# The second mixer's delta rule with its two token halves in one stage each

## What is computed

```
def step(state, inp):
    r_t, w_t, k_t, v_t, a_t, b_t = inp
    sa = jnp.einsum('bhvk,bhk->bhv', state, a_t)
    state = (state * w_t[:, :, None, :] + sa[..., None] * b_t[:, :, None, :]
             + v_t[..., None] * k_t[:, :, None, :])
    return state, jnp.einsum('bhvk,bhk->bhv', state, r_t)

_, y = lax.scan(step, jnp.zeros((B, H, d, d), jnp.float32), xs)
```

## Time and profile before

| what | value |
|---|---|
| median of 3 runs | 2688.8 us |
| the three runs | 2682.73, 2688.80 and 2691.91 us |
| the profiled execution's own time | 2688.18 us |
| its span | 2686.0 us |
| mean granted clock of TensorE in it | 0.96 |
| TensorE busy | 2472.5 us, 92% of the span |
| VectorE busy | 1835.3 us, 68% |
| ScalarE busy | 1307.8 us, 49% |
| GpSimd busy | 517.4 us, 19% |

### The profile page before, as it was taken

One profiled execution on the slowest core, in us unless ns is written; L12 is line 12 of the kernel. 1 busy time (PEld: TensorE's weight loads), 2 busy tenths in 40 slices (PEclk: granted clock), 3 DMA queues, 4 the chain that ended last, 5 costly groups with the idle time before them and its releaser, 6 DMA issues. The chain is left out here.

```text
span 2686.0 us, 47036 instructions
## 1 busy us (share of the span) xinstructions
PE 2472.5 (92%) x17864; PEld 2248.3 (84%) x17864; DVE 1835.3 (68%) x3790; ACT 1307.8 (49%) x1990; POOL 517.4 (19%) x328
## 2 busy tenths in 40 slices
PE   5698999999999999778999999999999987887999
PEld 4588999987878788668999998788887966786998
DVE  6775888768777776763888857666666456554754
ACT  3345664546544445454665456455545543044433
POOL 0001676623000000200576753000000020000000
PEclk8799999999999999789999999999999988899999
DMA  8755777772788776624677773577774531042554
GB/s 353 270 174 153 183 184 181 194 244 43 256 256 261 252 249 200 240 95 145 184 180 181 186 181 75 169 218 215 217 215 137 182 119 56 14 138 71 172 160 154
DMA packets 200517, 480.59 MB, mean 179 GB/s; under 512 B 54448, under 2 KB 87728, under 8 KB 199760
## 3 DMA queue, kind: packets, MB, share of 16 engines
q1 hardware_dynamic: 150960, 431.75, 50.7%
q10 hardware_dynamic: 12576, 47.29, 4.9%
q0 software_dynamic: 36864, 0.15, 3.5%
HBM read 461.15 MB, written 17.96 MB: 178 GB/s over the span
## 5 line engine op out<-in xcount | busy, mean ns | idle before, releaser
L278 DVE TENSOR_TENSOR weight_low<-weight_raw,weight_high 128x1024 fp32r<-128x1024 f32 x732 | 893.1, 1222 | 410.9 <-ACT weight_high L272 405.8
L272 ACT ACTIVATE weight_high<-weight_raw 128x1024 fp32r<-128x1024 f32 x732 | 773.8, 1059 | 690.9 <-DMA weight_raw<-peer_v_dram 344.3
L382 PE MATMUL bank<-h_high,weight_high 128*128 128x256 f32 x3424 | 981.5, 287 | 71.7 <-DVE h_low L537 21.7
L382 PE MATMUL bank<-h_low,weight_high 128*128 128x256 f32 x3424 | 978.3, 286 | 0.0
L382 PE MATMUL bank<-h_high,weight_low 128*128 128x256 f32 x3424 | 977.7, 286 | 0.0
L382 PEld LDWEIGHTS bank<-h_high,weight_high 128*128 128x128 f32 x3424 | 666.9, 195 | 84.1 <-issue 75.5
L382 PEld LDWEIGHTS bank<-h_low,weight_high 128*128 128x128 f32 x3424 | 666.8, 195 | 0.0
L382 PEld LDWEIGHTS bank<-h_high,weight_low 128*128 128x128 f32 x3424 | 666.7, 195 | 0.0
L1171 POOL DMA_INDIRECT gate_table<-pick_expo,pick_spot x256 | 474.3, 1853 | 667.3 <-DVE pick_expo L1273 390.6
L1452 PE MATMUL bank<-weight_high,act_high 128*128 128x512 f32 x1024 | 319.5, 393 | 9.8 <-DVE act_low L1519 6.1
L1452 PE MATMUL bank<-weight_low,act_high 128*128 128x512 f32 x1024 | 317.0, 391 | 0.0
(11 more groups left out here) (348 smaller groups left out, 2610.0 us busy)
## 6 DMA issues: line engine op xcount, KB each, us to landing
weight_raw<-peer_u_dram SPq DMA_DIRECT2D x256, 512.0 KB
weight_raw<-peer_v_dram SPq DMA_DIRECT2D x256, 512.0 KB
kept<-ada_later_dram ACTq DMA_DIRECT2D x54, 512.0 KB, 4.7
gate_table<-kept ACTq DMA_DIRECT2D x8, 2048.0 KB, 18.1
weight_raw<-peer_w_q_dram SPq DMA_DIRECT2D x32, 512.0 KB
kept<-gate_table SPq DMA_DIRECT2D x256, 64.0 KB, 4.3
weight_raw<-w_in_dram SPq DMA_DIRECT2D x32, 512.0 KB
weight_raw<-mlp_w_up_dram SPq DMA_DIRECT2D x32, 512.0 KB
```

What stands on the lines that cost most here:

```text
L272: self.nc.scalar.activation(self.high[:, slot, :], self.raw[:, slot, :], ACT.Identity) \
L278: eng.tensor_tensor(self.low[:, slot, :], self.raw[:, slot, :], self.high[:, slot, :].bitcast(F32), ALU.subtract) \
L382: mm = self.nc.tensor.matmul(out, w, x, start=(start and i == 0), stop=(stop and i == 2), skip_group_check=skip)
```

## The change

The function `tile` and its loop go. Each of the three blocks now exists once and works on both halves, so that six blocks become three. The tensors NT, LT, RB, RK, M1, inv and inv_T hold 16 heads instead of 8 (8t + h), and `both` moves to `spots[5]`, where a_in and b_out lie, which are no longer needed by then.

- Scores: the loop over the eight groups runs for t = 0 and then for t = 1, into the same eight banks. Group for group, TensorE waits before it writes a bank again until VectorE has read it. VectorE's 16 operations keep their size. GpSimd makes 32 copies in this block.
- Levels: the two groups that alternate are now the two halves with 8 heads each, instead of two groups of four heads within a half. A product is 16 matmuls instead of 8, and a VectorE operation 128x512 instead of 128x256. Six levels are gone through once instead of twice.
- Final products: every step is done for half 0 and then for half 1 before the next step begins, in other banks.

The number of matmuls, their size and their operands are the same. The core of the diff:

```diff
-    def tile(t):
...
+    with nc.Block() as block:
+        @block.tensor
+        def _(pe):
+            for t in range(TT):
                 for n, (left, right, _, _) in enumerate(kinds):
                     for g in range(2):
+                        if t:
+                            pe.wait_ge(out_ready.sem, out_ready.at(2 * n + g + 1))
                         for h in range(g, 8, 2):
...
-                        nc.vector.tensor_tensor(dst[:, g:8:2, :], half4(2 * n + g), mask(which), ALU.mult)
...
+                        dve.wait_ge(full.sem, full.at(8 * t + 2 * n + g + 1))
+                        nc.vector.tensor_tensor(product_of[:, 8 * t + g:8 * t + 8:2, :], half4(2 * n + g), mask(which, 4), ALU.mult) \
+                            .then_inc(out_ready.sem, 1)
+
+        @block.gpsimd
+        def _(pool):
+            for g in range(TT * 8):
+                nc.gpsimd.tensor_copy(inv[:, g, :], eye2)
+                nc.gpsimd.tensor_copy(inv_T[:, g, :], eye2)
...
+            def product(bank, left, right, t):
                 for h in range(8):
                     for c in range(2):
...
+                        mm = nc.tensor.matmul(core.bank[bank + 3 * t][rows(c), hc(h)], left[rows(c), 8 * t + h, :],
+                                              right[rows(c), 8 * t + h, :], start=True, stop=True, skip_group_check=True)
+                return mm
+
+            for level in range(6):
+                for t in range(TT):
+
+                    if level:
+                        pe.wait_ge(out_ready.sem, out_ready.at(4 * (level - 1) + 2 + t + 1))
+                    product(0, NT, inv, t).then_inc(full.sem, 1)
+                for t in range(TT):
+
+                    pe.wait_ge(out_ready.sem, out_ready.at(4 * level + t + 1))
+
+                    if 0 < level < 5:
+                        product(1, inv_T, M1, t)
+                    product(2, M1, inv_T, t).then_inc(full.sem, 1)
+
+        @block.vector
+        def _(dve):
+            for level in range(6):
+                for t in range(TT):
+                    dve.wait_ge(full.sem, full.at(4 * level + t + 1))
+                    nc.vector.tensor_tensor(M1[:, heads_of(t), :], eight(3 * t), mask(level, 8), ALU.mult).then_inc(out_ready.sem, 1)
+                for t in range(TT):
+                    dve.wait_ge(full.sem, full.at(4 * level + 2 + t + 1))
+                    own = heads_of(t)
+                    if level < 5:
+                        nc.vector.tensor_tensor(inv[:, own, :], inv[:, own, :], eight(1 + 3 * t) if level else M1[:, own, :], ALU.add)
+                    nc.vector.tensor_tensor(inv_T[:, own, :], inv_T[:, own, :], eight(2 + 3 * t), ALU.add).then_inc(out_ready.sem, 1)
...
+            for t in range(TT):
+                pe.wait_ge(out_ready.sem, out_ready.at(t + 1))
                 for g in range(2):
                     for h in range(4 * g, 4 * g + 4):
...
-                pe.wait_ge(out_ready.sem, out_ready.at(3))
+            for t in range(TT):
+                pe.wait_ge(out_ready.sem, out_ready.at(2 + 2 * t + 2))
                 for c in range(2):
+                    out = core.bank[2 + 2 * t + c]
...
+            for t in range(TT):
                 for c in range(2):
+                    out = core.bank[(6, 7, 0, 1)[2 * t + c]]
                     for h in range(8):
...
+            for chunk in range(CHUNKS):
+                sums = core.bank[2 + chunk]
+                dve.wait_ge(full.sem, full.at(6 + chunk + 1))
...
+            for chunk in range(CHUNKS):
+                dve.wait_ge(full.sem, full.at(10 + chunk + 1))
+                sums = core.bank[(6, 7, 0, 1)[chunk]][:].rearrange("p (o n k) -> p o n k", o=2, n=4)
...
-    for t in range(TT):
-        tile(t)
```

More of the change, by code:

```diff
@@ L2314, in rwkv @@
     full, out_ready = sig("products_ready"), sig("products_kept")
-    def tile(t):
[L2318 to L2329, removed]
+    half = lambda h: slice(64 * (h % 2), 64 * (h % 2) + 64)
@@ new lines, in rwkv @@
+    hc = lambda h: slice(h * 64, (h + 1) * 64)
+    rows = lambda c: slice(CHUNK * c, CHUNK * (c + 1))
+    of_chunk = lambda t, c: slice(t * P + CHUNK * c, t * P + CHUNK * (c + 1))
+    mask = lambda i, heads: masks[:, i, :].unsqueeze(1).to_broadcast([P, heads, CHUNK])
+    kinds = [(b_out, a_in, NT, 6), (k_out, a_in, LT, 6), (b_out, r_in, RB, 7), (k_out, r_in, RK, 7)]
+    bank4 = lambda i: core.bank[i][:].rearrange("p (h k) -> p h k", h=4)
+    eight = lambda i: core.bank[i][:].rearrange("p (h k) -> p h k", h=8)
@@ L2333, in _ @@
                             for c in range(2):
-                                mm = nc.tensor.matmul(core.bank[2 * n + g][rows(c), hc(h // 2)], left[half(h), h // 2, of_chunk(c)],
-                                                      right[half(h), h // 2, of_chunk(c)], start=True, stop=True, skip_group_check=True)
+                                mm = nc.tensor.matmul(core.bank[2 * n + g][rows(c), hc(h // 2)], left[half(h), h // 2, of_chunk(t, c)],
+                                                      right[half(h), h // 2, of_chunk(t, c)], start=True, stop=True, skip_group_check=True)
@@ L2345, in _ @@
[L2345 to L2388, removed]
@@ L2396, in _ @@
+    full.close(16)
+    out_ready.close(16)
+    with nc.Block() as block:
+        @block.tensor
+        def _(pe):
+            def product(bank, left, right, t):
                 for h in range(8):
                     for c in range(2):
[L2398 removed]
+                        mm = nc.tensor.matmul(core.bank[bank + 3 * t][rows(c), hc(h)], left[rows(c), 8 * t + h, :],
[11 more added lines that the diff above has]
+                    product(2, M1, inv_T, t).then_inc(full.sem, 1)
+        @block.vector
+        def _(dve):
+            for level in range(6):
[8 more added lines that the diff above has]
+                    nc.vector.tensor_tensor(inv_T[:, own, :], inv_T[:, own, :], eight(2 + 3 * t), ALU.add).then_inc(out_ready.sem, 1)
@@ L2399, in _ @@
+    full.close(24)
+    out_ready.close(24)
+    with nc.Block() as block:
+        @block.tensor
+        def _(pe):
+            for t in range(TT):
+                for h in range(8):
+                    for c in range(2):
+                        mm = nc.tensor.matmul(core.bank[t][rows(c), hc(h)], LT[rows(c), 8 * t + h, :], v_tok[rows(c), t, hc(h)],
                                               start=True, stop=True, skip_group_check=True)
                 mm.then_inc(full.sem, 1)
+            for t in range(TT):
@@ L2404, in _ @@
                         for c in range(2):
-                            nc.tensor.matmul(core.bank[1 + g][rows(c), at + 64:at + P], inv_T[rows(c), h, :], a_tok[rows(c), t, hc(h)],
-                                             start=True, stop=True, skip_group_check=True)
-                pe.wait_ge(out_ready.sem, out_ready.at(1))
+                            nc.tensor.matmul(core.bank[2 + 2 * t + g][rows(c), at + 64:at + P], inv_T[rows(c), 8 * t + h, :],
+                                             a_tok[rows(c), t, hc(h)], start=True, stop=True, skip_group_check=True)
+            for t in range(TT):
+                pe.wait_ge(out_ready.sem, out_ready.at(t + 1))
                 for g in range(2):
@@ L2423, in _ @@
                         at = slice(T + (h // 2) * 64, T + (h // 2) * 64 + 64)
-                        nc.tensor.matmul(core.bank[3 + c][half(h), at], b_tok[rows(c), t, hc(h)], both[rows(c), h, 0:64],
+                        nc.tensor.matmul(out[half(h), at], b_tok[rows(c), t, hc(h)], both[rows(c), 8 * t + h, 0:64],
                                          start=True, stop=False, skip_group_check=True)
-                        mm = nc.tensor.matmul(core.bank[3 + c][half(h), at], k_tok[rows(c), t, hc(h)], v_tok[rows(c), t, hc(h)],
+                        mm = nc.tensor.matmul(out[half(h), at], k_tok[rows(c), t, hc(h)], v_tok[rows(c), t, hc(h)],
@@ L2427, in _ @@
                                               start=False, stop=True, skip_group_check=True)
                     mm.then_inc(full.sem, 1)
+            for t in range(TT):
                 for c in range(2):
+                    out = core.bank[(6, 7, 0, 1)[2 * t + c]]
                     for h in range(8):
-                        at, out = (h // 2) * CHUNK, core.bank[5 + c]
-                        nc.tensor.matmul(out[half(h), at:at + CHUNK], both[rows(c), h, 64:P], RB[rows(c), h, :], start=True, stop=True,
-                                         skip_group_check=True)
+                        at = (h // 2) * CHUNK
+                        nc.tensor.matmul(out[half(h), at:at + CHUNK], both[rows(c), 8 * t + h, 64:P], RB[rows(c), 8 * t + h, :],
+                                         start=True, stop=True, skip_group_check=True)
@@ L2435, in _ @@
                         at += T
[L2436 to L2439, removed]
+                        nc.tensor.matmul(out[half(h), at:at + CHUNK], both[rows(c), 8 * t + h, 0:64], RB[rows(c), 8 * t + h, :],
```

(13 more changed lines are left out.)

44 lines of the change are left out of this document (27 added, 17 removed).

## The result

The changed kernel takes 2671.2 us in the median of 4 runs (2669.72 to 2671.89), the kernel before 2689.14 in the median of 4 (2682.73 to 2691.91). The ratio is 0.9949, its 95% interval 0.9932 to 0.9965: 13.7 us faster, anything from 9.4 to 18.3. The forecast was 2675.9 with a range of 2671 to 2683, so the time lies in the range, at its lower end. Two further comparisons of the same kernel gave 0.9953 and 0.9943.

The account below looks back on a forecast made before the run. The prediction took a chain passed to and fro between TensorE and VectorE as the bound on the delta-rule stretch. Savings of 2.25 + 4.6 + 6.0 = 12.9 us from the 2688.8 median gave 2675.9, range 2671 to 2683.

Parts of the forecast that it names:

- A microsecond saved in the stretch is one off the end: Second mixer's delta rule, 72.35 us: all that follows waits for it, so its whole saving shortens the kernel.
- Scores, 2.25: Scores stages: one block of 16 VectorE products takes 6.43 us instead of 8.68; 1.16 of the saving is half 1's clock.
- Levels, 4.6: Levels stages: both halves share each level's TensorE pause, 6.28 us a level against 6.82; 34.9 us instead of 39.5.
- rival (c): Levels: clock falls in their new pauses and stays low; 2699.5 us if three levels before their end; chance 0.03.
- Final products, 6.0: Final stages: one block takes 18.15 us instead of 24.16; 2.4 of the saving is the clock of half 1.
- Rival (a): Final products: clock falls inside, six of eight chunks at 1.2 GHz, 6.4 us of gain lost, 2682.3 us; chance 0.20.
- States stage, nothing: Stage behind the final products: could gain 1.8 us if the clock stays high; no gain was counted.
- Sum, 12.9: Whole delta-rule stretch: scores, levels and final products together save 12.9 us, from 72.35 to 59.5.
- Chances: Whole kernel, with about 0.3 per cent (8 us) needed to tell: faster 0.75, same 0.22, slower 0.03.
- Rival (b): Levels: a doubled level takes twice the old 3.41 us, so the 4.6 us goes, leaving 2680.5 us; chance 0.07.
- its other form: Levels: VectorE alone sets them, so its larger operations save 2.4 us instead of 4.6, time 2678.1 us; within the 0.07.

Follow-up runs that it names:

- scores_apart: Changed kernel with only the scores put back to a block for each half, 16 GpSimd copies each; stretch 60.39 us, ratio 0.9971 to the kernel before.
- final_apart: Changed kernel with only the final products put back to a block for each half; stretch 64.90 us, ratio 0.9972 to the kernel before.
- levels_apart: Changed kernel with only the levels put back to a block for each half, VectorE operations 128x256; stretch 65.52 us, ratio 0.9991 to the kernel before.
- split_ops: Changed kernel with each 128x512 VectorE operation in the levels split into two of 128x256; levels stage 37.26 us against 36.37.

## Why the prediction held, step by step

- **A microsecond saved in the stretch is one off the end**: held. From the end of the stretch to the end of the span it is 354.2, 352.8 and 350.9 us in the three traces of before, 353.0, 353.1 and 350.1 in the three of the changed kernel: no difference beyond their scatter, and the 1.1 us of the first pair belong to it.
- **Scores, 2.25**: 1.9 in the first pair of traces (8.68 to 6.78). The working missed the pause for instructions, which cost VectorE 0.35 there and 0.17 in the trace with the short pause. It called the waits for freed banks free, which they are; I looked for new waits in semaphores alone. Of the 2.25 only about 1 is the joining, the rest is the clock of half 1 before; scores_apart shows what it is worth where the clock holds, 7.53 against 6.60 to 6.83, and in two of three traces the fall behind the pause took more than that back.
- **Levels, 4.6**: 4.62 where the clock holds (39.51 to 34.89), 3.1 in the first trace. The term was right; the 1.5 us are level 0, half of it at 1.2 GHz: 7.41 us (36.37 less four times 6.27 and 3.88) instead of 5.9. That is rival (c) in small. It named the new pauses between levels as the danger; there the clock never fell, and what preceded the fall was the pause in the scores with the edge behind it.
- **Final products, 6.0**: 5.97, with two small misses that cancel. The state products began 6.33 us into the stage and not 6.1, and from VectorE's first read of a chunk to its last it was 9.40 and not 9.6: the reads of state products are 1.28 apart, and the 1.37 of the prediction was an average over three steps of which only one was such. The 3.6 of it that are pauses and edges came again in final_apart (3.7). The 2.4 of the clock were there in two of three traces of before. Rival (a) did not occur in any of the 11 traces with a joined or restored final stage after the change.
- **States stage, nothing**: 5.15 to 5.21.
- **Sum, 12.9**: 11.0 in the first pair, 12.9 in the trace in which nothing fell (59.47 against the 59.5 predicted), 10.9 over three traces each. The median moved by 17.9, and the 13.7 of the ratio has all of these within its interval. That the time lies 4.7 under the forecast is thus not more gain in the block: the traces place the rest ahead of it and behind it, where it comes and goes. That the median fell inside the range, by 0.2 us, is thus in part luck: by the ratio's 13.7 the time would have been near the forecast, by the median's 17.9 it is at the edge. The range had 3 us for the runs' scatter; 33 single executions spread over 19 us.
- **Chances**: 0.75 on faster by over 0.3 per cent; it was 0.5 per cent. Rival (b) fell with levels_apart, and its other form, that VectorE's larger operations are the gain, with split_ops.

What stays open: why the clock falls in level 0 in five traces of eight; that the pause is a wait for instructions, which the traces fit and do not prove; and where ahead of the block whole executions lose or win their 20 us.

## To carry to other kernels

Where two engines hand a dependent chain to and fro, put two independent chains through one stage: each pause is then paid once for both, and the gain can be worked out beforehand (34.9 us forecast for the levels, 34.89 measured where the clock held) from the pace of one group and the two hand-over times. Then look at what the waiting instruction really needs: one signal for two results held back 2.8 us here (60.39 to 57.62), where the joining of the levels had brought 4.6. And a change that makes an engine denser calls on what was never short before, here, as far as the traces tell, its supply of instructions.

## What the runs showed of the hardware that I had not expected

TensorE can stand still in straight code with no semaphore in its way: at 100 instructions a microsecond (64x64 matmuls with their weight loads) it stood still for 0.32 to 1.00 us at the same place of the stream in each of eight traces, and went on 1.2 to 1.4 us after a 16 KB transfer of instructions had landed; with half as many in one block (128 recorded matmul instructions) it did not stand still within a block. The 2250 us of unchanged instructions ahead of the block varied by 20 us, while the block itself repeated to 0.2 us where the clock did the same.
